# HGRN2 near scores in parts of two heads between the k tiles of the gate projection

## The reference, cut to what matters

```python
q, f_logit, i, g = jnp.split(xn @ w_in, 4, axis=-1)       # 8 heads of 128
f = lb + (1.0 - lb) * sigmoid(f_logit);  q = silu(q);  k = 1 - f
...
b = jnp.cumsum(log_f, axis=2)
decay = jnp.exp(where(causal, b_t - b_s, -inf))
scores = jnp.einsum('bhtk,bhtsk,bhsk->bhts', q, decay, k)
o = jnp.einsum('bhts,bhsv->bhtv', scores, v) + ...
o = rms_norm(o, o_gain).reshape(B, L, D) * sigmoid(g)
```

## Time and profile before

| | value |
|---|---|
| median of 3 runs | 1333.72 us (1332.06 to 1334.63) |
| profiled execution, its own time | 1337.42 us |
| span of the profiled execution | 1335.7 us |
| TensorE matmul busy | 1304.4 us, 98% |
| TensorE weight load busy | 1259.0 us, 94% |
| VectorE busy | 937.0 us, 70% |
| ScalarE busy | 627.6 us, 47% |
| chain that ended last | TensorE 78%, VectorE 9%, ScalarE 6%, DMA 4%, issue 2% |

### The profile page before, as it was taken

How to read it: one execution, slowest core, us unless ns; L and a number is a source line. 1 busy time by engine, 2 the same in 40 slices (tenths; PEclk the granted TensorE clock), 3 DMA queues, 4 the chain that set the end, 5 groups by cost and what they waited for, 6 DMA issues and landing times.

```text
span 1335.7 us, 27531 instructions
## 1 busy us (share of the span) xinstructions
PE 1304.4 (98%) x11142; PEld 1259.0 (94%) x11142; DVE 937.0 (70%) x1185; ACT 627.6 (47%) x728; POOL 60.3 (5%) x101
## 2 busy tenths in 40 slices
PE   9999999999999999999999999999998999999998
PEld 9998899999999999999999999999997899999986
DVE  7666688887567856888866776767874657976644
ACT  6365554344355245544443444434635564544533
POOL 3000000000012000000000000000010000000000
PEclk9999999999999999999999999999999999999999
DMA  7541255556655334455565678874584334565543
GB/s 285 193 154 64 96 195 183 193 184 218 238 171 191 129 110 164 171 186 188 198 245 185 237 276 271 299 248 177 176 286 158 117 135 160 194 222 183 186 160 124
DMA packets 40401, 252.27 MB, mean 189 GB/s; under 512 B 4544, under 2 KB 4800, under 8 KB 16144
## 3 DMA queue, kind: packets, MB, share of 16 engines
q1 hardware_dynamic: 29232, 211.89, 45.1%
q0 software_dynamic: 10816, 39.32, 8.6%
q10 hardware_dynamic: 288, 0.13, 0.0%
HBM read 250.27 MB, written 1.05 MB: 188 GB/s over the span
## 4 chain that ended last, share of the span: by engine, by line
PE 78%; DVE 9%; ACT 6%; DMA 4%; issue 2%; SPq 0%; DVEq 0%; ACTq 0%; POOLq 0%
PE ps L2220 63%; PE ps L2871 4%; DVE w_lo L1131 4%; ACT w_hi L477 3%; PE ps L2241 2%; DMA raw<-in_units_mix_in 1%; DMA raw<-in_units_glu_up 1%; PE ps L2564 1%; PE ps L2441 1%; DMA raw<-in_units_ffn_up 1%; PE ps L2613 1%; PE ps L2374 1%; PE ps L2667 1%; ACT scratch L702 1%; PE ps L2333 0%
## 5 line engine op out<-in xcount | busy, mean ns | idle before, releaser
L2220 PE MATMUL ps<-x_hi,w_hi 128*128 128x258 f32 (+2 forms) x1984 | 568.5, 287 | 3.9 <-DVE x_lo L1297 1.1
L2220 PE MATMUL ps<-x_hi,w_lo 128*128 128x258 f32 (+2 forms) x1984 | 563.5, 284 | 0.0
L1131 DVE TENSOR_TENSOR w_lo<-raw,w_hi 128x2048 fp32r<-128x2048 f32 (+1 forms) x183 | 438.9, 2398 | 171.3 <-ACT w_hi L477 169.6
L477 ACT ACTIVATE w_hi<-raw 128x2048 fp32r<-128x2048 f32 (+1 forms) x183 | 365.9, 1999 | 391.5 <-PE ps L2220 286.9
L2220 PE MATMUL ps<-x_lo,w_hi 128*128 128x258 f32 (+2 forms) x1824 | 518.7, 284 | 0.0
L2220 PEld LDWEIGHTS ps<-x_hi,w_hi 128*128 128x128 f32 x1984 | 374.7, 189 | 8.8 <-issue 1.9
L2220 PEld LDWEIGHTS ps<-x_hi,w_lo 128*128 128x128 f32 x1984 | 375.1, 189 | 0.0
L2220 PEld LDWEIGHTS ps<-x_lo,w_hi 128*128 128x128 f32 x1824 | 343.6, 188 | 0.2
L2220 PE MATMUL ps<-g_hi,w_hi 128*128 128x256 f32 (+1 forms) x576 | 163.2, 283 | 2.1 <-DVE w_lo L1131 1.1
L2220 PE MATMUL ps<-g_hi,w_lo 128*128 128x256 f32 (+1 forms) x576 | 162.8, 283 | 0.0
L2220 PE MATMUL ps<-g_lo,w_hi 128*128 128x256 f32 (+1 forms) x576 | 162.2, 282 | 0.0
(11 more groups left out here) (382 smaller groups left out, 1640.2 us busy)
## 6 DMA issues: line engine op xcount, KB each, us to landing
raw<-in_units_ffn_up SPq DMA_DIRECT2D x44, 1024.0 KB, 4.9
raw<-in_units_glu_up SPq DMA_DIRECT2D x44, 1024.0 KB, 5.0
v_tok<-in_w_ada_t POOLq DMA_DIRECT2D x72, 512.0 KB, 4.4
raw<-in_units_ffn_down SPq DMA_DIRECT2D x16, 1408.0 KB, 5.9
raw<-in_units_mix_in SPq DMA_DIRECT2D x20, 1024.0 KB, 5.0
raw<-in_units_hgrn_in SPq DMA_DIRECT2D x16, 1024.0 KB, 4.9
raw<-in_units_fox_in SPq DMA_DIRECT2D x14, 1024.0 KB, 5.0
raw<-in_units_glu_down SPq DMA_DIRECT2D x8, 1408.0 KB, 5.9
```

Of the source, the lines that this page charges most:

```text
L477: nc.scalar.activation(w_hi[s][:, 0:size], raw[s][:, 0:size], ACT.Copy).then_inc(hi_ready, 1)
L1131: V.tensor_tensor(w_lo[s][:, 0:size], raw[s][:, 0:size], w_hi[s][:, 0:size].bitcast(F32), ALU.subtract).then_inc(lo_ready, 1)
L2220: ins = T_.matmul(dst, fixed, moving, start=(kt == 0 and i == 0), stop=(kt == kts - 1 and i == 2))
```

## The change

`gemm` gets a callback `mid_kt`, called behind each k tile. `near_scores(l, part)` now makes two heads (18 matmuls, 16 in level 5); parts 0 and 1 are group 0, parts 2 and 3 group 1. The waits stand ahead of the even parts, the count `lv_used` behind the odd ones, and `lv_taken` 3 is waited for ahead of part 0 of level 3 alone. The level of tile n is issued as: part 0 behind k tile 5 of tile n, part 1 behind its last k tile, part 2 behind k tile 1 and part 3 behind k tile 3 of tile n + 1. VectorE, ScalarE, GpSimd and SP programs are the same.

```diff
-            def gemm(name, xw, xh, xl, T, k=None, after=None, late=None, mid=None, packed=False, outer=None, resume=False, by_tokens=(), its=None):
+            def gemm(name, xw, xh, xl, T, k=None, after=None, late=None, mid=None, packed=False, outer=None, resume=False, by_tokens=(), its=None, mid_kt=None):
...
                                         ins = T_.matmul(dst, fixed, moving, start=(kt == 0 and i == 0), stop=(kt == kts - 1 and i == 2))
+                                    if mid_kt:
+                                        mid_kt(it, s, m, kt)
...
-            def near_scores(l, g):
-
-                if l == 0:
-                    pe.wait_ge(f_ready, 1)
-                    pe.wait_ge(gates_done, 6 + 2 * g)
-                else:
-                    pe.wait_ge(lv_ready, 2 * (l - 1) + g + 1)
-                if l == 3:
-                    pe.wait_ge(lv_taken, 3)
+            def near_scores(l, part):
+
+                g = part // 2
+                if part % 2 == 0:
+                    if l == 0:
+                        pe.wait_ge(f_ready, 1)
+                        pe.wait_ge(gates_done, 6 + 2 * g)
+                    else:
+                        pe.wait_ge(lv_ready, 2 * (l - 1) + g + 1)
+                    if l == 3 and g == 0:
+                        pe.wait_ge(lv_taken, 3)
                 at = l % 3 * (2 * ROWS_32 + META)
-                for h1 in range(4 * g, 4 * g + 4):
+                for h1 in (2 * part, 2 * part + 1):
...
-                ins.then_inc(lv_used, 1)
+                if part % 2:
+                    ins.then_inc(lv_used, 1)
...
+            def level_of(n):
+                return n if n < 3 else n - 1 if 4 <= n < 7 else None
+
+            def in_g(it, s, m, kt):
+
+                n = 4 * it + 2 * s + m
+                if kt == 5 and level_of(n) is not None:
+                    near_scores(level_of(n), 0)
+                if kt in (1, 3) and n and level_of(n - 1) is not None:
+                    near_scores(level_of(n - 1), 2 + kt // 2)
+
             def between_g(it, s, m):
 
                 n = 4 * it + 2 * s + m
-                if n < 3:
-                    near_scores(n, 0)
-                    near_scores(n, 1)
-                elif 4 <= n < 7:
-                    near_scores(n - 1, 0)
-                    near_scores(n - 1, 1)
+                if level_of(n) is not None:
+                    near_scores(level_of(n), 1)
...
-            gemm("hgrn_in", from_norm(2), xh_used, xl_used, L - UNUSED, k=2, mid=between_g)
+            gemm("hgrn_in", from_norm(2), xh_used, xl_used, L - UNUSED, k=2, mid=between_g, mid_kt=in_g)
```

## The result

The changed kernel takes 1339.71 us (median of 9 runs, 1337.66 to 1346.25) beside 1334.31 us for the one before in the same runs (1332.06 to 1336.77): a ratio of 1.004, with a 95% interval of 1.0028 to 1.0052. It is slower by 5.4 us, and the interval stands for 3.7 to 6.9 us.

A forecast was written before the change was run, and what follows sets the result against it. TensorE, its matmuls busy for 98% of the span, was taken as the bound. Edges +5.3, stops -1.8 and VectorE's turn +1.9 sum to +5.4 us on 1333.7, giving 1339.1 us, range 1335.0 to 1342.6.

The forecast's parts named there:

- the likeliest case: Whole kernel: the forecast itself, a time of 1337 to 1341 us, chance 0.68.
- No cover behind the stretch: TensorE from 463 to 500 us has no idle time, so time lost or gained earlier carries to the end one for one.
- Edges, +5.3: Switches between projection and small products: 18 more insertions at 0.295 us each add 5.3 us.
- Stops, -1.8: TensorE's code stops in levels 0 and 1, 2.2 us: the first goes, 0.4 of the second stays, saving 1.8 us.
- VectorE's turn, +1.9: TensorE waits for later VectorE work: level 3 0.65, tile 6 0.95, level 6 group 1 0.3; together 1.9 us.
- Hidden edges: Rival: short parts between k tiles pay little for the switch; 1333.8 to 1335.6 us, chance 0.13.
- the edge that belongs to the burst's length: Rival: short parts pay no edge and the six now paid go too; -4.0 us with both stops gone, 1329.7, chance 0.04.
- Late pieces: Rival: later code pieces meet weight transfers, two meetings adding 1.4 to 3.0 us; 1340.5 to 1342.1 us, chance 0.15.

The follow-up runs named there:

- 24 and 48 insertions: Against the kernel before: four two-head parts behind k tiles 4 to 7 of the level's own tile, 1338.68 us; eight parts of one head, 1348.21 us.
- whole-array product: Kernel before plus one spare two-record fp32 product of the whole array at 15 places between projection matmuls; 1339.36 us in one run.
- 18 more products: Kernel before with the first two heads' products of level 0 made twice; 1342.08 us beside 1335.11, ratio 1.0047.
- One edit: The change with VectorE's w_lo split of unit 3 moved ahead of decay(4, 1); 1340.42 us beside 1335.11 for the kernel before, ratio 1.0042.
- one-head parts: Against the kernel before: eight parts, behind k tiles 4 to 7 of the level's tile and 0 to 3 of the next; 1348.21 us, ratio 1.0098.
- moved bursts: Kernel before with whole bursts moved: level 0 behind k tile 3 of tile 1, level 2 behind k tile 3 of tile 3; 1334.44 us, ratio 0.9999.
- one-tile kernel: Kernel before plus one spare two-record fp32 product of a 32-column tile at 15 places between projection matmuls; 1347.95 us in one run.

## Why the prediction was right

The forecast was 1339.1 us and +5.4; measured are 1339.7 and +5.4, inside the range and the likeliest case. The mechanism was right in its three terms. That the sum agrees to 0.1 us is partly luck: the runs leave 3.7 to 6.9 us open, and two errors in the term for the stops cancel. Point by point:

- *No cover behind the stretch.* +5.3 in the stretch, +5.4 (3.7 to 6.9) in the runs: nothing of size is given back.
- *Edges, +5.3.* Shown at 18, 36, 72 and 144 records, and by 24 and 48 insertions (49.3 and 56.8 us). The reason I put beside it was half of it. The Trainium skill (TensorEngine Tiling (Array Packing), Key Properties) has a drain at a change of tiling mode; the entry's 0.10 us comes with the tile size and not with a whole-array product, which agrees. The larger half, at the way back to the projection, comes for the most part with a short whole-array product too, so that rule doesn't cover it. A third of the edge, the last 0.10, comes with a new start of the projection, behind a code stop too; what makes the part between wasn't separated.
- *Stops, -1.8.* -1.8 measured from start to start, though neither number under it was right: the two stops cost 2.55 us and not the 2.2 that their idle time gave, and 0.72 stayed where I had 0.4. The position was right: the stop that is left stands where 256 instructions put it. That the pieces are of 256 instructions is shown by the stops that moved with 18 more products. The Trainium skill (Runtime: NRT & Kernel Launch, Instruction fetch mechanics) gives that size, and the runs agree; its "mostly hidden" doesn't hold in this stretch, with stops of 0.3 to 3.5 us in eleven of the twelve kernels profiled.
- *VectorE's turn, +1.9.* 1.8 measured, at the three places named: 0.53 (0.65 foreseen), 0.93 (0.95) and 0.35 (0.3). One edit removed one of them.
- *The rivals.* Hidden edges and the edge that belongs to the burst's length both fall with the change's own parts and with the one-head parts. Late pieces didn't come in the change itself beyond the one foreseen. The 18 more products, with 5.5 us in the stretch, show how easily they could have: that none did isn't something that the forecast had worked out.
- *Two wrong terms in later expectations.* That a level has the same stops wherever its code begins (18 more products: at most +0.8 foreseen, +5.5 in the stretch), and that moved bursts leave the late pieces behind (43.3 to 44.0 foreseen, 44.8).

## What to carry to other kernels

Count how often TensorE changes between a stream of projection matmuls and small products, and not only how many products there are: here 0.3 us an insertion, as much as 30 records of small products. A stop marked "issue" in the midst of a run of short matmuls is worth counting in instructions; if such stops are a fixed count apart (here 128 matmul records and as many weight loads), it's the code that is late, and any edit ahead of it moves them, so that the time of a small edit there says little of the edit itself. Compare the same stretch in two traces before two spans: the spans of these differed by 0.8 us where the runs differed by 5.4.

## What the runs showed of the hardware

A stop ends 2.2 to 2.7 us behind the start of its 16 KB instruction packet, in all 25 stops. A packet is late above all when a weight transfer is under way: for 20 of the 25, weights were being moved in the microsecond ahead of it. In the kernel before, the two packets stand at 433.5 and 438.8 us, and 0.33 and 0.43 MB of weights were moved in the microsecond ahead of them. In the kernel before and with 18 more products the second stop ended at 441.08 and 441.12 us, although TensorE had come to it 0.25 us sooner (439.37 + 0.79 against 439.25 + 1.16). The four longest stops (1.48, 1.52, 2.13 and 3.46 us) are all of this kind. The other five stops, of 0.26 to 0.98 us, have no weight transfer in the 3 us ahead of the packet, and why those packets are late stays open.

A stop can also cost more than itself. The kernel with 18 more products, around its 2.13 us stop (windows as above):

```profile
460.00:464.00 4.00, 4.00 (x137) 3.83 (x127) 4.00 (x4) 1.10 (x2) 0.00 (x0) 1.00 0.66 248
464.00:468.00 4.00, 1.87 (x54) 1.76 (x43) 3.73 (x8) 0.42 (x2) 0.00 (x0) 0.79 0.54 174
468.00:472.00 4.00, 4.00 (x29) 4.00 (x28) 2.61 (x5) 3.55 (x9) 0.00 (x0) 0.78 0.27 111
```

TensorE was busy for 1.87 of 4 us, and then the granted clock fell to 1.2 GHz for part of two windows (0.79 and 0.78 on the mean):

```profile
467.38 0.42 PE L2220 MATMUL ps<-x_hi,w_hi 128*128 128x258 f32 x1
467.60 0.42 PE L2220 MATMUL ps<-x_lo,w_hi 128*128 128x258 f32 x1
...
470.13 0.28 PE L2220 MATMUL ps<-x_hi,w_lo 128*128 128x258 f32 x1
470.25 0.28 PE L2220 MATMUL ps<-x_hi,w_hi 128*128 128x258 f32 x1
```

Projection matmuls start 0.22 us apart there and 0.12 later. From 466.57 to some 469.8 us that are 14 of them, 1.4 us lost behind the stop. From start to start its four stops cost 1.63, 1.16, 1.25 and 2.20 us, 6.2 together, less 2.55 before. So the 5.5 us of that kernel are 0.4 of products, 3.7 of stops and 1.4 of clock. The one-tile kernel shows the same behind its 3.46 us stop: from 475.55 to 478.64 us its projection matmuls start 0.20 to 0.23 us apart. The same stands in the profiled execution of the kernel before at 1024 to 1032 us, behind 4 us in which it was busy for 2.00. The 1.5 us stop of level 0 was followed by no such fall in the two profiles that have it.
